# A decode attention loop: keys turned by VectorE in 32x32 blocks, scores as products in sixteen array tiles, and pages laid on 32 partitions in 4 KB packets

## The reference

```python
# per sampled token b: 16 heads, past of 2048 positions in 16 pages of 128
c   = cache_ckv[page_table[b]]     # (2048, 256) latent, pages gathered from a pool
kpe = cache_kpe[page_table[b]]     # (2048, 32)  rotary key
s = einsum('bqhr,bkr->bhqk', q_lat, c) + einsum('bqhe,bke->bhqk', q_pe, kpe)
p = softmax(concat([s * scale, own position's score]))
out = einsum('bhqk,bkr->bqhr', p, c) + own position's share
```

## Time and profile before

| | |
|---|---|
| median of three runs | 2008.1 us (2007.0, 2008.1, 2010.79) |
| the profiled execution: its span | 2007.1 us, 41,612 instructions |
| busy over the span | PE 98%, DVE 64%, ACT 41%, POOL 7% |
| granted TensorE clock | nine tenths or more of full speed in all 40 slices |
| DMA | 211.55 MB, mean 105 GB/s |
| decode loop, first to last maximum | 1510.63 to 1578.47 us: 67.84 us for seven items |

### The profile page before, as it was taken

The page is one execution under the profiler, slowest core; times in us unless marked ns, Lnnn a source line. Parts: engine busy times, 40 slices in busy tenths (PEclk is TensorE's granted clock), DMA queues, the critical chain, the costliest instruction groups (busy, mean ns, idle before and its releaser), DMA issues.

```text
span 2007.1 us, 41612 instructions
## 1 busy us (share of the span) xinstructions
PE 1960.4 (98%) x17604; PEld 1875.2 (93%) x17604; DVE 1277.0 (64%) x1771; ACT 820.4 (41%) x1243; POOL 132.8 (7%) x231
## 2 busy tenths in 40 slices
PE   8999999988999999999999999999989999999999
PEld 7999999987999999999999999997666799999998
DVE  6445486697469577576884856655764349668474
ACT  5332233343245244255452534454654244345252
POOL 3002002010000000000000000000047000000000
PEclk9999999989999999999999999999999999999999
DMA  7233234864342322234322322231248422323222
GB/s 151 84 102 88 75 93 115 269 140 100 95 137 85 120 89 95 77 105 116 97 85 85 127 85 86 84 101 51 54 119 231 149 71 83 127 85 120 91 74 75
DMA packets 260624, 211.55 MB, mean 105 GB/s; under 512 B 42372, under 2 KB 235426, under 8 KB 260450
## 3 DMA queue, kind: packets, MB, share of 16 engines
q1 hardware_dynamic: 248528, 187.52, 31.9%
q0 software_dynamic: 6656, 13.69, 2.4%
q10 hardware_dynamic: 5266, 7.85, 1.2%
HBM read 195.29 MB, written 10.33 MB: 102 GB/s over the span
## 4 chain that ended last, share of the span: by engine, by line
PE 67%; DVE 3%; ACT 2%; issue 2%; SPq 1%; DMA 1%; DVEq 0%; ACTq 0%
PE ps L2459 25%; PE ps L2487 25%; PE ps L2388 6%; PE ps L2401 2%; PE ps L2947 1%; PE ps L3053 1%; PE ps L3209 1%; PE ps L3086 1%; SPq L654 1%; SPq L639 1%; DMA cb<-cache_ckv 1%; PE ps L2841 1%; PE ps L3030 1%; DVE wl L1668 0%; DVE xl L1619 0%
## 5 line engine op out<-in xcount | busy, mean ns | idle before, releaser
L2388 PE MATMUL ps<-xh,wh 128*128 128x260 f32 x1088 | 286.9, 285 | 2.6 <-DVE xl L1619 1.4
L2388 PE MATMUL ps<-xl,wh 128*128 128x260 f32 x1088 | 283.7, 283 | 0.0
L2487 PE MATMUL ps<-xoh,wh 128*128 128x260 f32 x992 | 281.3, 284 | 1.3 <-DVE sq L1835 1.3
L2487 PE MATMUL ps<-xoh,wl 128*128 128x260 f32 x992 | 281.0, 283 | 0.0
L2487 PE MATMUL ps<-xol,wh 128*128 128x260 f32 x992 | 280.6, 283 | 0.0
L2459 PE MATMUL ps<-xh,wh 128*128 128x260 f32 x872 | 228.8, 284 | 0.6 <-DVE wl L1668 0.6
L1067 ACT ACTIVATE wh<-rw 128x1024 fp32r<-128x1024 f32 (+1 forms) x135 | 138.8, 1029 | 218.6 <-PE ps L2459 151.7
L2459 PE MATMUL ps<-xl,wh 128*128 128x260 f32 x872 | 227.0, 282 | 0.0
L2388 PE MATMUL ps<-xh,wl 128*128 128x260 f32 x1088 | 219.3, 283 | 0.0
L990 ACT ACTIVATE wh<-raw 128x1024 fp32r<-128x1024 f32 (+1 forms) x90 | 100.4, 1116 | 283.4 <-PE ps L2388 250.5
L2388 PEld LDWEIGHTS ps<-xh,wh 128*128 128x128 f32 x1088 | 205.6, 189 | 6.9 <-issue 3.9
(11 more groups left out here) (550 smaller groups left out, 4202.2 us busy)
## 6 DMA issues: line engine op xcount, KB each, us to landing
rw<-ffn_w_gate SPq DMA_DIRECT2D x33, 1024.0 KB, 5.4
rw<-ffn_w_up SPq DMA_DIRECT2D x33, 1024.0 KB, 8.0
rw<-ffn_w_down SPq DMA_DIRECT2D x12, 2048.0 KB, 7.8
raw<-ffn_w_gate SPq DMA_DIRECT2D x22, 512.0 KB, 3.9
raw<-ffn_w_up SPq DMA_DIRECT2D x22, 512.0 KB, 3.9
raw<-ffn_w_down SPq DMA_DIRECT2D x16, 704.0 KB, 4.8
rw<-ffn_w_down SPq DMA_DIRECT2D x6, 1536.0 KB, 6.7
cb<-cache_ckv SPq DMA_DIRECT2D x72, 128.0 KB, 3.7
```

Of the source, the lines that this page charges most:

```text
L2388: got = mm(ps[0:width, bank + half, 0:HALF], w[par_][:, k * width:k * width + width], src[:, k0 + k, half * HALF:half * HALF + HALF], star ...
L2487: got = mm(ps[:, bank + mat, T0], w[:, cols], src[:, j, k, :], start=first and k == 0 and m == 0 and s == 0, stop=k == 3 and m == 1, skip_ ...
```

## The change

- **Layout of the loads.** `page_rows(buf, g)` puts page g on only 32 partitions, 32(g % 4) to 32(g % 4)+31; each of these takes four positions of the page, 4 KB in one piece of memory (kpe: 512 B). The number of DMAs, of bytes and of issuing engines stays.
- **Turning.** PE makes no transposes of keys and ACT no copies of them. DVE does it with `V.transpose`, which transposes 32x32 blocks, from SBUF to SBUF: per item one over 128x512 (kpe) and four over 128x1024 (`TURN_W` = 2 blocks of 32 ranks each).
- **Scores.** `cache_scores(b, q)`: after the block transposes 32 ranks lie on each group of 32 partitions. For kpe 16 products (K = 32, 32 weight columns), for each of the eight blocks of ranks 16 products (K = 32, 16 weight columns), all of 128 columns, each in one of the 4x4 tiles of 32x32 of the array: 144 products per item. Row group g writes PSUM bank 4+g. There is one such set of banks, so that the first product of item b+1 waits for the exponential of b.
- **Queries.** The weights must lie on each of the four row groups: `qrep` is filled by 16 more DMAs on POOL, SBUF to SBUF, before the cache loads' DMAs on that queue.
- **Moves.** The copy to `pbT` goes from DVE to ACT. PE's order is now: turns of pb(b), cache_scores(b+1, 0), weighted sum of b, cache_scores(b+1, 1 to 4). DVE's is: turned(b+1, 0), maximum of b, its scaling, turned(b+1, 1 to 4). turned(b+1, 0) waits for all the data of item b+1. `keys(b)` waits for the first turned piece of item b-3. In the prompt's last pair of heads PE no longer has the nine pieces of item 0's turning; DVE has item 0's instead.

```diff
+                return buf[P // NQ * (g % NQ):P // NQ * (g % NQ + 1), NQ * (g // NQ):NQ * (g // NQ + 1), :]
...
-                    eng.wait_ge(d_t, 9 * (b - 2))
+                    eng.wait_ge(d_t, TURNS * (b - 3) + 1)
...
-                    eng.dma_start(cb[j][:, g, :], inp["cache_ckv"][bass.ds(numbers[b][g], 1)].rearrange("a p r -> p (a r)")).then_inc(arrived[j], 16)
+                    eng.dma_start(page_rows(cb[j], g), inp["cache_ckv"][bass.ds(numbers[b][g], 1)].rearrange("a (p t) r -> p (a t) r", t=NQ)).then_inc(arrived[j], 16)
...
-                run(pb, ps[:, 2 + b % 2, :], ACT.Exp, bias=nmb[:, b:b + 1], scale=SCALE, accum_out=lb[:, b:b + 1]).then_inc(d_e, 1)
-                if b + 1 < NB:
-                    for q in range(2, 9, 2):
-                        turned(b + 1, q)
+                run(pb.rearrange("p (s g t) -> p g s t", s=NQ, g=NQ), sc.rearrange("p g (s t) -> p g s t", s=NQ), ACT.Exp,
+                    bias=nmb[:, b:b + 1], scale=SCALE, accum_out=lb[:, b:b + 1]).then_inc(d_e, 1)
+                act.wait_ge(d_pt2, b + 1)
+                if b >= 1:
+                    act.wait_ge(d_o, b)
+                run(pbT[:, :, :], ps[:, PT_BANK, :].rearrange("p (m q) -> p m q", m=NQ), ACT.Copy).then_inc(d_pe, 1)
...
+                if q == 0:
+                    dve.wait_ge(d_in[j], (b // 3 + 1) * 16 * N_SP)
+                    dve.wait_ge(d_kin[j], (b // 3 + 1) * 16 * N_POOL)
...
+                if q == 0:
+                    V.transpose(kbT, kb[j][:, :, :]).then_inc(d_t, 1)
+                else:
+                    cols = slice(RG * TURN_W * (q - 1), RG * TURN_W * q)
+                    V.transpose(cbT[:, :, cols], cb[j][:, :, cols]).then_inc(d_t, 1)
...
             for b in range(NB):
+                if b + 1 < NB:
+                    turned(b + 1, 0)
                 dve.wait_ge(d_s, b + 1)
-                own(V.tensor_reduce(mb[:, b:b + 1], ps[:, 2 + b % 2, :], AX.X, ALU.max))
+                own(V.tensor_reduce(mb[:, b:b + 1], sc, AX.XY, ALU.max))
...
+            def cache_scores(b, q):
+
+                pe.wait_ge(d_t, TURNS * b + q + 1)
+                if q == 0 and b == 0:
+                    pe.wait_ge(d_qr, 16 * NQ * NQ)
+                    pe.wait_ge(a_ol, NH // 2)
+                elif q == 0:
+                    pe.wait_ge(d_e, b)
+                for k in range(TURN_W * (q - 1), TURN_W * q) if q else (NRB,):
+                    for g in range(NQ):
+                        rows = slice(RG * g, RG * (g + 1))
+                        for c in range(NQ):
+                            pages_ = slice(NQ * c, NQ * (c + 1))
+                            if k < NRB:
+                                heads, w, src = NH, qrep[rows, k % NQ, k // NQ, b, :], cbT[rows, pages_, RG * k:RG * (k + 1)]
+                            else:
+                                heads, w, src = HP, qpe[rows, b, g, :], kbT[rows, pages_, :]
+                            got = mm(ps[HP * c:HP * c + heads, SC_BANK + g, 0:P], w, src, start=q == 0, stop=k == NRB - 1, skip_group_check=True)
+                got.then_inc(d_sp if q < NTP else d_s, 1)
...
+            pool.wait_ge(l_qe, 1)
+            for g in range(NQ):
+                for k in range(NQ):
+                    pool.dma_start(qrep[RG * g:RG * (g + 1), k, :, :, :], qlat[RG * k:RG * (k + 1), :, :, 0:NH]).then_inc(d_qr, 16)
```

More of the change, by code:

```diff
@@ L71 @@
 KB = PAST // NQ
+RG = P // NQ
+NRB = R // RG
+TURN_W = 2
+NTP = NRB // TURN_W
+TURNS = NTP + 1
+SC_BANK, PT_BANK = 4, 3
 NEG = -1e30
@@ L2269, in _ @@
                 else:
-                    turned(0, 1)
+                    turned(0, 0)
                 probs(i, 5)
@@ L2277, in _ @@
                     normalise(i + 1, 3)
-            turned(0, 3)
-            turned(0, 5)
+            turned(0, 1)
             weighted(NH // 2 - 1)
-            turned(0, 7)
+            for q in range(2, TURNS):
+                turned(0, q)
             def wide_lo(j):
@@ L3185, in _ @@
                 turned_probs(i, 3)
-                if not more:
-                    turned(0, 0)
                 turned_probs(i, 4)
-                if not more:
-                    turned(0, 1)
                 turned_probs(i, 5)
@@ L3193, in _ @@
                     values(i // 2 + 1, i % 2)
-            for q in range(2, 6):
-                turned(0, q)
             weighted(NH // 2 - 1)
-            for q in range(6, 9):
-                turned(0, q)
             def wo_half(d, half, k0, k1):
@@ new lines, in weighted_rows @@
+            def weighted_rows(b):
+                pe.wait_ge(d_pe, b + 1)
+                if b >= 2:
+                    pe.wait_ge(d_oe, b - 1)
+                for m in range(NQ):
+                    for c in range(NQ):
+                        got = mm(ps[HP * c:HP * c + HP, 1 + b % 2, 0:R], pbT[:, m, HP * c:HP * c + HP], cb[b % 3][:, 4 * c + m, :],
+                                 start=m == 0, stop=m == NQ - 1, skip_group_check=True)
+                got.then_inc(d_o, 1)
+            for q in range(TURNS):
+                cache_scores(0, q)
@@ L3248, in _ @@
                     turn(ps[0:NB, 7, P:2 * P], lb[:, :]).then_inc(d_rt, 1)
+                    pe.wait_ge(d_oe, NB - 1)
                     wo_half(1, 0, 0, 3)
-                pe.wait_ge(d_pe, b + 1)
-                if b >= 2:
-                    pe.wait_ge(d_oe, b - 1)
-                elif b == 1:
-                    pe.wait_ge(a_ol, NH // 2)
-                for m in range(NQ):
-                    for c in range(NQ):
-                        got = mm(ps[HP * c:HP * c + HP, 5 + j, 0:R], pbT[:, m, HP * c:HP * c + HP], cb[b % 3][:, 4 * c + m, :],
-                                 start=m == 0, stop=m == NQ - 1, skip_group_check=True)
-                got.then_inc(d_o, 1)
+                weighted_rows(b)
+                if b + 1 < NB:
+                    for q in range(1, TURNS):
+                        cache_scores(b + 1, q)
             wo_half(1, 0, 3, KD)
+            pe.wait_ge(d_oe, NB)
             wo_half(2, 0, 0, 3)
```

94 lines of the change are left out of this document (21 added, 73 removed).

## The result

| | before | after |
|---|---|---|
| median | 2007.95 us (4 runs, 2007.0 to 2010.79) | 2045.49 us (4 runs, 2043.06 to 2046.85) |
| ratio | 1 | 1.017, 95% interval 1.015 to 1.0189 |
| profiled span | 2007.1 us | 2044.4 us |
| instructions | 41,612 | 44,797 |
| DVE's maxima in the loop, first and last | 1510.63, 1578.47 | 1514.97, 1614.30 |

The change costs 37.5 us by the medians, and 1.5 to 1.9%, 30 to 38 us, by the interval of the ratio, where 4 us of gain was forecast. In the profiled executions (37.3 us) 4.3 us arise before the first maximum, 99.33 - 67.84 = 31.5 us in the seven items, and 1.5 us behind them. So the loop is the question.

What follows compares the result with a forecast made beforehand. SP's DMA issues, 9.7 us an item, were taken as the bound, with PE at 9.5 before. Start -1.3, last landing -1.0 and tail -1.9 made -4.2 us: span 2002.9, median 2003.9 us, range 1997 to 2016.

Steps and rivals of the forecast that it cites:

- the period of the loop: Decode loop: PE's cycle without the data's wait takes 7.0 us an item, hidden under SP's 9.7 us of issues.
- 16 tiles at once would be a quarter: Score products: 8 ns a record taken, bounds 7.7 and 31, part of -1.9 us from last data to last maximum.
- rival 4: Score products: sixteen tiles don't run together as hoped; at 14.8 ns a record period 8.8 us, total 2005.7; chance 0.12.
- Scores of q = 1 to 4: Latent's score products of an item on PE: 256 records, 0.5 us for each quarter of the ranks.
- the mix of four pages in flight would not: Cache loads: a single page onto 32 partitions lands slower, but four pages together use all ports and don't.
- The rival: Cache loads onto 32 partitions are slower, 226 to 233 GB/s, 10.1 to 10.4 us an item, about 2008; chance 0.10.
- The start: Before the loop: without item 0's turning on PE, pages(2) and the chain of issues come 1.3 us earlier, bounds 0 and -2.0.
- a transpose of 1024 elements on DVE: Turning of the latent on DVE: 1.2 us each taken, bounds 0.6 and 2.4, four an item.
- the issue of a page: SP's load issues: 0.570 us a DMA kept, 9.7 us an item; whether the 0.33 us issue falls with 32 packets, unshown.
- qrep's DMAs: 16 DMAs on POOL after qlat is filled: over by some 1402 us, 100 us ahead of the first score, costing nothing.
- Rival 2: Decode loop: PE idles 5 us an item and its clock falls to half; centre 2008 us, in full 2021; chance 0.15.
- The range from the terms' bounds: Total time from the bounds of start, last landing and tail, without the rivals: 2001 to 2007 us.

Runs made afterwards that it cites:

- x15: x10 with two products of 512 columns filling PE's wait for the exponential; 2012.20 us, ratio 1.0006.
- x14: The kernel before with 40 useless short products (80 records) more an item on PE; 2014.54 us, ratio 1.0019.
- x9: The kernel before with 84 useless short products (168 records) more an item on PE; 2036.75 us, ratio 1.012.
- x3: The changed kernel with score products joined in pairs, 72 of 256 columns instead of 144 of 128; 2018.34 us, ratio 1.0039.
- x1: The kernel before with only the loads changed, each page on 32 neighbouring partitions in 4 KB packets; 2019.18 us, ratio 1.0053.
- x2: The changed kernel with the loads of before, 1 KB on each of 128 partitions; 2031.84 us, ratio 1.0118.
- x11: x2 with the quarters of the weighted sum alternating with the four bursts of scores on PE; 2035.54 us, ratio 1.0122.
- x8: The changed kernel with the loads of before and PE's wait for the exponential filled as in x5; 2031.89 us, ratio 1.009.
- x5: The changed kernel with two products of 512 columns filling PE's wait for the exponential in the first seven items; 2048.34 us, ratio 1.0171.
- x6: The changed kernel with each ckv DMA of items 3 to 7 cut to a quarter of its bytes; 2030.34 us, ratio 1.0087.
- x4: The changed kernel with the latent's score products cut to 32 of 128 columns, same instruction count; 2043.01 us, ratio 1.0172.
- x10: The changed kernel with score products joined as in x3 and the loads of before; 2014.17 us, ratio 1.0014.

## Why the prediction was wrong

The bound was read right for the kernel before, and for a loop like the one forecast (x15: 9.62 us an item, data late). The step that failed is the period of the loop, 7.0 us for PE's cycle, of which the prediction says "It is under SP's 9.7, so that nothing is won in it": it left the instruction stream out and took the loads at their old rate, and 14.19 us were measured. By its terms:

- **"16 tiles at once would be a quarter, 7.7 ... I take 8 to start with".** The term of the scores was mis-sized: 14.5 ns a record, the bound that I had and put in a rival, from the earlier trace rows. 256 records take 3.7 us, not 2.0. Alone, that would have stayed under SP's time (rival 4: 8.8 us).
- **"Scores of q = 1 to 4: 4 x 64 records" was priced by the array and the issue alone.** The fetching of the instructions stood at nothing, without a reason, and no rival had it. What the runs showed in its place are 20.5 us of pauses at boundaries of 128 records. An item goes from 120 to 324 records, and from x14 (200) to x9 (288) the cost goes from 4 to 25 us. This is the larger cause (26 us in x3). The trace of before had the hint: instruction packets of 16 KB, one to an item of 120 records.
- **"the mix of four pages in flight would not"** land slower. It does: 217 GB/s at a share of 1.03 where before moved 230 at 0.79, 291 at a full share: 10 us in before (x1), 10 to 14 in the changed kernel (x2). The rival had the mechanism at 226 to 233 GB/s and a price of 4 us, with 0.10 of the chance; the earlier trace rows showed that rate for two small loads.
- **The start, -1.3 us.** In the profiled execution pages(2) came 2.0 us later instead, at 1509.18 against 1507.16. This isn't the change's doing, nor DVE's turned(0, 0), which ended at 1504.18, when PE's transposes for the last copy had only just ended (1504.17). PE was 0.4 us late at 1384 us and 3.45 us late at 1412, ahead of all that the change does to PE, and between lies a stretch at half clock. Windows of PE there, of the changed kernel, of before, of x15 and of x14:

```profile
1387.00:1393.80 6.80, 6.80 (x37) 4.94 (x36) 1.75 (x2) 0.58 (x4) 3.96 (x7) 0.50 0.15 21
```

```profile
1387.00:1393.80 6.80, 6.25 (x38) 3.75 (x39) 1.72 (x3) 2.23 (x6) 0.00 (x0) 1.00 0.00 0
```

```profile
1387.00:1393.80 6.80, 6.25 (x40) 3.75 (x40) 1.71 (x3) 2.23 (x6) 5.11 (x8) 1.00 0.21 29
```

```profile
1387.00:1393.80 6.80, 6.25 (x43) 4.59 (x44) 2.03 (x3) 1.40 (x6) 0.00 (x0) 0.75 0.00 0
```

x14 has the kernel before up to here, x15 the changed one: the stretch comes in some executions of both and not in others. Among the variants of the changed kernel without it, pages(2) starts at 1505.58 (x11), 1505.99 (x15) and 1506.71 (x8), 1.6, 1.2 and 0.5 us before 1507.16. The term was about right, and some us of any single profile's total are the execution's own.
- **Right**: a transpose of 1024 elements on DVE takes 1.21 us (1.2 taken), of 512 0.70; the issue of a page stays at 0.32 to 0.33 us with 32 packets; the weighted sum and turns at full clock; qrep's DMAs cost nothing that shows.
- **Rival 2, the clock.** It came, 0.70 from 1520 to 1580, for the reason given, idle PE. But as long as the stream waits little of its price was seen (x5 none, x8 6 us by the ratios with 0 inside the intervals).
- **The range from the terms' bounds** was added up a little wrong: -2.0, -2.1 and -1.9 against 0, 0 and -0.2 from 2008.1 are 2002.1 to 2007.9 us, not 2001 to 2007. Nothing hangs on it at 2045.5.

Open: what makes one fetch take so long. A packet itself takes 0.96 to 2.13 us in the changed kernel's loop. That it is more than the traffic, x6 shows; no run changed the fetch itself, so that the link from fetch to pause rests on the count of the instructions (x3, x4, x9, x14) and on the packets' times.

## What to carry to other kernels

Count instructions an item before splitting products: 256 of PE's come in one packet, and here the next one was ready only 4 us or more later, so that bursts which use up a packet sooner stand still, whatever the array's work. Short products in small tiles are cheap only as long as few of them follow each other. Before a microsecond or two of a single profile is explained, compare the granted clock ahead of the stretch. Lay a load over partitions that are spread, but look at what the issue then costs, since the gain of one can be the loss of the other.

## What the runs showed of the hardware

- PE paused 0.9 to 5.1 us at boundaries of 256 instructions, with nothing else awaited, when an item of 12 to 14 us held 288 to 324 product records (after, x2, x9), and not at all with 200 in 10.06 us (x14). In after and x9 each pause ended 0.9 to 1.7 us after the end of a 16 KB packet of the instruction queue. The Trainium skill's page "Runtime: NRT & Kernel Launch", section "Instruction fetch mechanics", has instructions fetched in blocks of 256 and calls the crossing of a boundary "mostly hidden". The blocks agree with the 128 records, and their 128 weight loads, between two pauses; the crossing is hidden in before, x10 and x14, and in none of the runs with 288 records or more.
- Records of 32x16 tiles came 14.5 ns apart with 128 columns and 11.3 ns apart with 32 (1.86 and 1.44 us for 128): a quarter of the columns saves a fifth of the time.
- The granted clock near 1388 us was half in some executions and full in others, of the kernel before (x14, before) as of the changed one (after, x15); across it the changed kernel's lateness against before grew from 0.4 us (1384) to 3.45 us (1412).
- 4 KB packets onto 32 neighbouring partitions took 82 us of engine time per MB, onto 32 spread ones 52, 1 KB onto 128 partitions 56. The issue of the spread ones took 0.68 us a DMA against 0.50.
